# Two layers whose first product group takes unscaled x, with the norm's path beside it

## The reference, cut to what matters

```
for l in range(2):
    shift, scale, gate = split(silu(c) @ w_ada[l] + b_ada[l], 3)
    h = rmsnorm(x, norm_g[l]) * (1 + scale) + shift
    z = h @ w_in[l]                    # 2048 -> 13 pieces of 512 columns
    ... four mixers on the pieces, each times silu(its gate) ...
    x = x + gate * (concat(...) @ w_out[l])
return rmsnorm(x, final_g)
```

## Time and profile before

| | us |
|---|---|
| median of three runs | 3087.59 |
| the three runs | 3082.22, 3087.59, 3087.74 |
| the profiled execution | 3084.55 |
| its span | 3082.7 |
| busy TensorE, weight load | 3047.6 (99%), 2691.3 (87%) |
| busy VectorE, ScalarE, GpSimd | 1930.9 (63%), 1446.8 (47%), 1291.7 (42%) |
| HBM read | 655.47 MB, 213 GB/s over the span |

### The profile page before, as it was taken

The page is one execution under the profiler, slowest core; times in us unless marked ns, Lnnn a source line. Parts: engine busy times, 40 slices in busy tenths (PEclk is TensorE's granted clock), DMA queues, the critical chain, the costliest instruction groups (busy, mean ns, idle before and its releaser), DMA issues.

```text
span 3082.7 us, 46476 instructions
## 1 busy us (share of the span) xinstructions
PE 3047.6 (99%) x18814; PEld 2691.3 (87%) x18814; DVE 1930.9 (63%) x2824; ACT 1446.8 (47%) x1877; POOL 1291.7 (42%) x643
## 2 busy tenths in 40 slices
PE   8999999999999999999999999999999999999998
PEld 7888888888899999998888888888899998899986
DVE  4777675673323446686567666555479864589764
ACT  5444444444657455544544444444444454544444
POOL 5454545445566555594554454444610004510013
PEclk9999999999999999999999999999999999999999
DMA  7888887886676555565788888787566545565454
GB/s 224 281 273 263 271 278 251 288 281 182 212 169 183 159 166 145 147 178 192 235 270 266 281 266 266 262 286 262 176 183 190 158 139 198 173 188 178 151 170 165
DMA packets 486655, 662.73 MB, mean 215 GB/s; under 512 B 67993, under 2 KB 273545, under 8 KB 486185
## 3 DMA queue, kind: packets, MB, share of 16 engines
q1 hardware_dynamic: 480952, 655.05, 66.8%
q0 software_dynamic: 4448, 2.94, 0.4%
q10 hardware_dynamic: 1040, 1.78, 0.2%
HBM read 655.47 MB, written 2.10 MB: 213 GB/s over the span
## 4 chain that ended last, share of the span: by engine, by line
PE 97%; DVE 1%; ACT 1%; issue 0%; DMA 0%; POOL 0%; ACTq 0%; DVEq 0%
PE ps L921 36%; PE ps L849 23%; PE ps L926 18%; PE ps L855 12%; PE ps L839 1%; PE ps L880 1%; PE ps L1357 1%; PE ps L1147 1%; PE ps L1128 1%; DVE narrow_split_slabs L1846 0%; PE ps L980 0%; PE ps L1055 0%; PE ps L1185 0%; PE ps L1155 0%; PE ps L1177 0%
## 5 line engine op out<-in xcount | busy, mean ns | idle before, releaser
L800 POOL TENSOR_TENSOR split_slabs<-stage,split_slabs 128x1024 fp32r<-128x1024 f32 x318 | 772.9, 2432 | 1320.6 <-ACT split_slabs L1412 1320.5
L1412 ACT ACTIVATE split_slabs<-stage 128x1024 fp32r<-128x1024 f32 x592 | 626.7, 1060 | 878.5 <-PE ps L926 844.7
L921 PE MATMUL ps<-split_slabs,h_split 128*128 128x512 f32 x3312 | 824.6, 391 | 0.9 <-ACT split_slabs L1412 0.9
L1412 ACT ACTIVATE narrow_split_slabs<-stage 128x1024 fp32r<-128x1024 f32 (+1 forms) x440 | 459.9, 1051 | 643.9 <-PE ps L855 564.7
L849 PE MATMUL ps<-h_split,narrow_split_slabs 128*128 128x256 f32 x5856 | 750.2, 281 | 0.0
L921 PEld LDWEIGHTS ps<-split_slabs,h_split 128*128 128x128 f32 x3312 | 622.4, 188 | 134.3 <-issue 5.1
L849 PEld LDWEIGHTS ps<-h_split,narrow_split_slabs 128*128 128x128 f32 x5856 | 704.4, 189 | 15.7 <-issue 12.3
L1846 DVE TENSOR_TENSOR split_slabs<-stage,split_slabs 128x1024 fp32r<-128x1024 f32 x274 | 349.5, 1276 | 527.3 <-ACT split_slabs L1412 526.0
L800 POOL TENSOR_TENSOR narrow_split_slabs<-stage,narrow_split_slabs 128x1024 fp32r<-128x1024 f32 (+1 forms) x181 | 435.4, 2415 | 314.7 <-ACT narrow_split_slabs L1412 307.1
L926 PE MATMUL ps<-split_slabs,h_split 128*128 128x512 f32 x1656 | 442.9, 389 | 0.3 <-POOL split_slabs L800 0.3
L1846 DVE TENSOR_TENSOR narrow_split_slabs<-stage,narrow_split_slabs 128x1024 fp32r<-128x1024 f32 x259 | 338.3, 1308 | 160.0 <-ACT narrow_split_slabs L1412 159.1
(11 more groups left out here) (254 smaller groups left out, 2098.7 us busy)
## 6 DMA issues: line engine op xcount, KB each, us to landing
stage<-in_w_in SPq DMA_DIRECT2D x360, 512.0 KB, 3.7
stage<-in_ffn_w_gu SPq DMA_DIRECT2D x352, 512.0 KB, 4.8
U<-in_w_ada SPq DMA_DIRECT2D x192, 512.0 KB, 5.4
stage<-in_ffn_w_down SPq DMA_DIRECT2D x176, 512.0 KB, 5.2
stage<-in_w_out SPq DMA_DIRECT2D x96, 512.0 KB, 4.2
stage<-in_w_in SPq DMA_DIRECT2D x80, 128.0 KB, 2.8
stage<-in_w_branch_c SPq DMA_DIRECT2D x32, 192.0 KB, 3.3
stage<-in_cmp_w SPq DMA_DIRECT2D x8, 512.0 KB, 5.6
```

What stands on the lines that cost most here:

```text
L800: nc.gpsimd.tensor_tensor(slab_part(n, 1, size(n)), stage[:, n % RING, 0:size(n)], slab_part(n, 0, size(n)).bitcast(F32), ALU.subtract).th ...
L921: mm(ps[:, 2 * pair + T, :], stationary(kk, i)[:, T * P:(T + 1) * P], w[0][:, kk, :], start=first and kk == 0 and i == 0, stop=False)
L1412: return fn(slab_part(n, 0, size(n)), stage[:, n % RING, 0:size(n)], ACT.Copy)
```

## The change

In each layer l the first group multiplies `raw_split[l]`, the split of the transposed x times `ascale`, which needs no rstd. For layer 0 this lies in `h_split`'s own place, for layer 1 in a region of U.

- Blocks 0 to 2 of x are transposed on VectorE while the product before the layer still runs (`turn_block`), rounded on ScalarE (`round_raw`) and subtracted on VectorE (`rest_raw`). For layer 0 this stands in the second feed-forward's down products, for layer 1 in layer 0's output product. Block 3 is transposed by TensorE behind the first slab of the group.
- `shift_sum` makes shift times W for the first 256 columns: a 2 MB load of these columns (`load_first_w`), then 16 VectorE instructions, each on the result of the one before, and two one-column matmuls.
- r is spread over the partitions by one fp32 matmul (`side_bank`), and `first_evacuate` puts r and the shift's share on the group's result.
- The norm's own path (`scale_x`, `turn_scaled`, `gain_h`, `split_h`) now feeds the second group. Its transposes stand between the slabs of the first group, the last one in the second group.
- Slabs 2 to 7 of each layer get their remainders from GpSimd in place of VectorE (`FIRST_POOL` = 8). GpSimd's wait for layer 1's scaled x is gone, and its constant load and bias loads come behind slab 7.

```diff
+RAW = LV
+FIRST_W = (SILU, UPAD - S * 4)
+FIRST_POOL = 8
+SHIFT_AT = (21, 23, 24, 29)
...
-        by_vector |= {n for l in range(2) for n in range(S_LAY[l] + 2, S_LAY[l] + 4 * PIECE)}
+        by_vector |= {n for l in range(2) for n in range(S_LAY[l] + FIRST_POOL, S_LAY[l] + 4 * PIECE)}
...
+                    if f == 1 and i == FFN_SLABS - 6:
+                        sp.wait_ge(ada_red, 2 * ADA_GROUPS)
+                        sp.wait_ge(act_turned, 2 * GU_GROUPS)
+                        load_first_w(0)
...
-                if n == S_LAY[1] + 1:
-                    pool.wait_ge(*scaled.after(4, 1, 1))
...
+            def raw_product(l, g, n):
+                r = 3 + l
+                pe.wait_ge(evacuated, g - 1)
+                for k in range(4):
+                    pe.wait_ge(*h_ready.after("raw", l, k))
+                    split_passes(acc(g), n + k, chunks_of(raw_split[l], k), k == 0, k == 3).then_inc(slab_done, 1)
+                    if k == 0:
+                        pe.wait_ge(*x_half.after(r))
+                        turn(1, 3, x, 0)
+                        pe.wait_ge(evacuated, X_READY[r])
+                        turn(1, 3, x, 1).then_inc(*turned.mark("raw", l))
+                    else:
+                        turn_scaled(r, k - 1)
+                    if k == 1:
+                        pe.wait_ge(*vec_out.after("rdiag", l))
+                        mm(side_bank(l)[:, S:2 * S], ones, u(LNX, P, S), start=True, stop=True)
...
             for l in range(2):
                 s0, g0 = S_LAY[l], G_LAY[l]
-                round_upto(s0 + 1 - l)
+                round_upto(s0 + 1)
                 squares(3 + l, 3)
+                round_upto(s0 + 2)
                 rstd_of(3 + l)
-                round_upto(s0 + 2)
+                round_raw(l, 3)
                 for b in range(4):
+                    round_upto(s0 + 3 + b)
                     gain_h(3 + l, b, ascale[:, l, :], mod[:, l, 0:16])
-                    if b == 2:
-                        round_upto(s0 + 3)
+                round_upto(s0 + 7)
...
+            def rest_raw(l, b):
+                for half in range(2):
+                    dve.wait_ge(*rounded.after("raw", l, b, half))
+                    for c in range(2):
+                        m = 4 * b + 2 * half + c
+                        src = turn_bank(1, 3, half)[:, c, :] if b == 3 else raw_plain(l, m)
+                        last = v.scalar_tensor_tensor(raw_split[l][:, 1, m, :], src, ascale[:, l, m:m + 1],
+                                                      raw_split[l][:, 0, m, :].bitcast(F32), ALU.mult, ALU.subtract)
+                last.then_inc(*h_ready.mark("raw", l, b))
...
-                for b in range(3):
+                scale_x(r, 0)
+                for T in range(TT):
+                    last = v.tensor_scalar(u(LNX, P, TT, P)[:, T, :], ident, rstd[:, r, T:T + 1], None, ALU.mult)
+                last.then_inc(*vec_out.mark("rdiag", l))
+                rest_raw(l, 3)
+                for b in range(1, 4):
                     scale_x(r, b)
                 split_h(r, 0)
-                scale_x(r, 3)
-                slab_lo(s0 + 2)
+                dve.wait_ge(*pe_out.after("shift", l))
...
                         if i == OUT_DONE[p] + 1:
                             residual(p)
                             if p + 2 < OUTG:
                                 diagonal(p + 2)
+                        if l == 0 and OUT_DONE[p] + 1 <= i < OUT_DONE[p] + 5:
+                            turn_block(4, p, i - OUT_DONE[p] - 1)
+                        if l == 0 and i == OUT_DONE[p] + 6:
+                            rest_raw(1, p)
+                    if l == 0 and i in SHIFT_AT:
+                        first = 4 * SHIFT_AT.index(i)
+                        shift_sum(1, first, first + 4)
```

138 lines of the change are left out of this document (95 added, 43 removed).

## The result

| | before | after |
|---|---|---|
| median | 3082.5 (five runs) | 3101.08 (five runs) |
| lowest and highest | 3079.48, 3087.74 | 3095.86, 3103.66 |
| profiled execution, its span | 3084.55, 3082.7 | 3103.66, 3101.8 |

The change makes the kernel slower: the ratio is 1.0052, with a 95% interval of 1.0041 to 1.0064, that is 18.6 us on the medians and 19.1 on the two spans. One execution of the last experiment, the profiled one, took 14753.07 with its matmuls of L968 at 1526 ns in place of 389, so that kernel has no stretches, and only its ten other runs say how long it takes.

What follows compares the result with a forecast made beforehand. The prediction took TensorE, busy 99% of the span, to bound the kernel. From 3084.55, -2 and 0 at the starts and +15 in layer 0's output product gave 3097.6, plus 1 for spread: 3098.5, range 3083 to 3106.

Steps and rivals of the forecast that it cites:

- The case on which it rested: VectorE's list in layer 0's output product gets too long and TensorE waits; 3093 to 3101, chance 0.55.
- the sum: Whole kernel: 3084.55 - 2 + 0 + 15 = 3097.6 on the profiled execution, plus 1 for the spread of runs.
- the two starts: Starts of layers 0 and 1: a gain of 2 and 0, with bounds -4 and +15.6 for both together.
- The output product: Layer 0's output product: slab 31's remainder comes 15 later, from VectorE's new work and its waits for the port.
- the "20": Layer 0's output product: the loss in place of 15 if every GpSimd slab holds the port for its full 2.4.
- Rival 3: Layer 0's output product: slab 19's wait puts TensorE at half speed, 2 to 8 more, 3101 to 3107; chance 0.10.
- the step that priced layer 0's `shift_sum` as hidden: Second feed-forward's down products: 16 instructions, 8.2 of VectorE work, taken to cost nothing there.
- At the starts the clock stays at 1.00: Both layer starts: TensorE keeps its full clock and the wait for the scaled x, 7.7 before, is gone.
- The waits in the second group: Layer starts: TensorE waits for the split blocks (L1891), 1 to 2 several times, each beside a GpSimd subtraction.
- The preparation of layer 0 and the loads at nothing: Second feed-forward's down products: transposes, roundings, subtractions and shift_sum cost nothing; the 2 MB load 0, at most 2.
- the pace named as a term without sign: Nine groups behind a start: 2.83 or 2.72 a slab, so 4 either way if the pace changes.
- Rival 1: Whole kernel: starts gain fully and VectorE keeps up in the output product; 3071, chance 0.13.

Runs made afterwards that it cites:

- the last experiment: Against the changed kernel: slabs 2 to 7 by VectorE, slab 19's remainder earlier, layer 1's shift share in three pieces at slabs 8, 10, 12; 3076.49, ratio 0.9973.
- the list made short: The changed kernel with layer 1's shift share made on only 8 of its 256 columns; 3096.16, ratio 1.0035.
- GpSimd held: The changed kernel, but GpSimd waits for rstd before the third slab of each layer; 3100.32, ratio 1.0055.
- the first slabs by VectorE: The changed kernel, but slabs 2 to 7 of each layer get their remainders from VectorE, as before the change; 3088.05, ratio 1.0016.

## Why the prediction was right, and where it wasn't

Forecast 3098.5, range 3083 to 3106, slower with 0.65; measured 3101.08. The case on which it rested came true. As a difference it was further off than the two times look: the sum added 13 to the profiled execution, and the two profiled executions differ by 19.1. Of the 6 between them 4.1 lie in the two starts, whose terms were mis-sized, and 2.3 in the rest of layer 1.

**The output product: right, 15 against 14.9.** VectorE is busy 64.49 of 66.00, slab 19's wait was forecast as 6.3 and is 6.05, and TensorE's first pass with slab 31's remainder comes 15.4 later than in the earlier trace rows, 14.8 when counted from the product's first matmul. With the transposes and most of the share left out, VectorE is busy 33.45 of 54 and the loss is zero. The make-up was right too. From slab 19's subtraction on the sum had 31.6 of work and 10.7 in six waits for the port, and an end at 2645.5; the trace has 41.0, that is 9.4 beyond the work, in five waits, and an end at 2645.57. Only the "20" with every GpSimd slab in full is a slip: 31.6 and seven times 2.4 behind 2603.2 end 21.4 later than 2630.23.

Rival 3 had the half clock behind a wait in mid-product, at 2 to 8. It came and cost TensorE 3.0, but the product ends when VectorE's list does, so it added nothing to the forecast; that much of it would be hidden is what the rival said itself. With the list made short it shows, 1.4 beside the wait. The Trainium skill's two states by recent activity (TensorE: Matmul & The Clock Gate, "What's actually happening"), cited beside that rival, agree: the clock was 0.53 around the end of the wait of 6.05.

**The starts: the sign was wrong.** Forecast -2 and 0, measured +0.8 and +1.3, terms off by 4.1 together. The mechanism I named, VectorE and GpSimd excluding each other on the port, is the one that the kernels with GpSimd held and with the first slabs by VectorE confirm. What was mis-sized is the time of rstd.

In layer 0 it had rstd at 2196.0 and it came at 2200.5. Of these 4.5, 2.4 (2192.90 for the second half's addition, 2190.47 before) come from the step that priced layer 0's `shift_sum` as hidden: its last four instructions took 6.08, ran past TensorE's end and held up the addition of x. The rest is a second GpSimd slab in the Newton steps: I had one there, but ScalarE had the slab after it rounded sooner than I assumed, and it came 0.19 behind the first. In layer 1 rstd was to come 6.7 behind the last wide matmul (2638.5 - 2631.82) and came 10.4 behind it (2657.72 - 2647.36). 1.8 of that is ScalarE's new list, the rounding and the table load ahead of the squares, for which the sum had nothing; the rest is again the second GpSimd slab.

From rstd on the sum came out, 24.5 less 1.5 is 23.0, measured 22.4, but in part by luck. It counted 12.5 of VectorE's work on the port and 12.0 for five GpSimd slabs. Four slabs were left, and VectorE stood 7.4 for them (2.05, 1.06, 2.06 and 2.20 over the times of the same instructions with the first slabs by VectorE); its own work was 15.0, because what needs no port, such as the last raw block and the copies from PSUM, takes its time all the same.

**"At the starts the clock stays at 1.00": wrong.** The wait for the scaled x did not go: TensorE stood 4.07 and 3.95, and the eight transposes behind took 1.92 and 1.74 for the 1.04 of later ones, with a granted clock of 0.54 from 2201.0 to 2203.5. The waits in the second group are nearly as forecast: 2.9 in four waits for L1891, the longest 1.1.

**The preparation of layer 0 and the loads at nothing: right but for the late x.** TensorE reaches the start of layer 0 at 2190.13, before at 2190.05, and has no new wait up to there.

**Not in the sum.** The trace of after has 2.3 more in the rest of layer 1. This is the pace named as a term without sign, 4 at most.

**Rival 1**, that it does what it says, did not come. The clean starts do win 4.8 each against the kernel before, once GpSimd is out of them, and the whole change with the share in the gaps is 8.8 faster than before. What decided was who subtracts which slab, and when.
